# Turned x and the first gate weights in shared transfers, x itself later, in a two-block transformer kernel

## The chip, the cores and the metric

The kernel runs on one core of one Trainium2 chip. The metric is the device time of one execution in microseconds (us), lower is better.

## The reference

Two blocks run one after the other on 256 tokens of width 1024, in float32, each block with two layers. What the change touches is only the very first part, the first feed-forward part of the first layer of the first block:

```
h = x
h = h + 0.5 * swiglu(rmsnorm(h, ffn1_norm[0]), w_gate, w_up, w_down)

swiglu(x, w_gate, w_up, w_down) = (silu(x @ w_gate) * (x @ w_up)) @ w_down
rmsnorm(x, g) = x * rsqrt(mean(x * x) + 1e-6) * g
```

`w_gate` and `w_up` are 1024 x 2816, `w_down` is 2816 x 1024. After it come a mixer of three branches, a second feed-forward part, the second layer, and then the second block with mixers and feed-forward parts of its own.

## The kernel before

**Numbers.** Each float32 product is made of three TensorE passes. A matrix is split into a high half (the value rounded to the fast format, `fp32r`, by ScalarE) and a low half (the value minus the high half, by VectorE). The three matmuls are low weights by high x, high weights by high x, and high weights by low x.

**Weight units.** All weights come in units, numbered j in the order in which they are used. A unit is one transfer from DRAM by SyncE into `raw[j % 6]`; ScalarE writes the high half into `wh[j % 5]` (line 1850), VectorE the low half into `wl[j % 6]` (line 2062). `raw[i]` and `wl[i]` are the same memory, so the fetch of unit j waits until TensorE is done with unit j - 6, and the high half of unit j waits until it is done with unit j - 5 (`NL, NH = 6, 5`, line 29). A unit is used in two visits, one for each half of the tokens (t = 0 and 1).

**Written-out order.** One planner, the class `Plan`, writes a single list of items; each engine's program walks through that list and executes its own items in that order. So the order on an engine is the order of the list. `group` (line 511) makes the TensorE items of some units and calls `tick` after each visit. `tick` (line 477) does three things in order: it runs what was put off, it moves each of four lanes of generators one step (`pump`, line 459), and it calls `advance` (line 427), which appends fetches whose buffer has been given back, low halves for high halves already listed, and high halves. In the opening `advance` lists high halves only up to three units ahead of the unit in use:

```
            if self.head < 14 and self.nhi > self.head + 3:
                break
```

**The opening.** In the first column chunk (512 gate columns, then 512 up columns) the reduction over 1024 is cut into eight k-tiles of 128. Gate comes as units of 1, 1, 1, 1, 2, 2 k-tiles (units 0 to 5), up as units of 2, 2, 4 (units 6 to 8). Later chunks have units of four k-tiles; unit 9 is the first gate unit of the second chunk. Units 0 to 3 are "fresh" (line 1595): TensorE takes high by high as soon as both high halves are there, then the low half of x, then the low half of the weights. All other units wait for the low half of the weights first.

The first feed-forward part doesn't wait for the norm: x comes turned (features on partitions) in an array `xg`, which also holds the gain, and is scaled by the gain while it is split (lines 1844, 2055 and 2057, one "slot" for each k-tile). The roots of the mean squares are applied later, as a scale in silu (line 1858) and in the product with up (line 2069). They come from x in its plain layout (`h`, loaded at line 1476): ScalarE squares and sums it (line 1884), GpSimd makes the root (lines 1510 and 1514).

`start` (line 844) lists the opening: transfers of units 0 to 5 with `xg` in three pieces between them (slots 0 and 1, 2 and 3, 4 to 7), then x in its plain layout, the identity for transposes, 16 filler matmuls for TensorE (line 1641), then the splits of x and of units 0 to 4. `opening` (line 870) is a lane: after five steps it lists the squares and roots, 14 steps later the loads of constants by GpSimd (lines 1527 to 1532). `silu_t` (line 729) lists silu at once, behind the visit that ends the gate sum.

Of the kernel before, what the change touches and what calls it, by code (L numbers as in the profile page):

```python
# [17 lines left out]
P = 128  # L18
D = 1024
S = 256  # L20
# [8 lines left out]
NL, NH = 6, 5  # L29
# [38 lines left out]
class Memory:  # L68


    def __init__(self, nc, A, out, ctx):
        self.nc, self.A, self.out, self.ctx = nc, A, out, ctx
        self.sbuf()
        s = self.sem
# [17 lines left out]
        self.fill_set = s("fill_set")  # L92
        self.xt_landed = [s(f"xt_landed{i}") for i in range(3)]
        self.x0_high = s("x0_high")
# [45 lines left out]
    def sbuf(self):  # L140
# [11 lines left out]
        A = self.at  # L152
# [45 lines left out]
        o_g = [rt(8192), rt(8192)]  # L198
        self.GT = [A(f"G{i}", o_g[i], [P, 8 * S]) for i in range(2)]
        o_lane = [rt(3584) for _ in range(3)]  # L200
        self.fill = A("fill", o_g[0] + 4096, [P, P], F32R)
        self.xg = A("xg", o_g[1] - 32, [P, 8 + 8 * S])
        self.gcol = self.xg[:, 0:8]
        self.xT = self.xg[:, 8:].rearrange("p (s n) -> p s n", n=S)
        self.lS = [[A(f"lS{i}{j}", o_lane[i] + 1536 * j, [P, 384]) for j in range(2)] for i in range(3)]
# [86 lines left out]

    def halves(self, j):
        kt, n = self.unit(j)
        return self.raw[j % NL][:, 0:kt * n], self.wh[j % NH][:, 0:kt * n], self.wl[j % NL][:, 0:kt * n]

# [75 lines left out]
class Plan:  # L372
# [54 lines left out]
    def advance(self, most=NL):  # L427
        while self.fetched < self.total and (self.fetched < NL or self.fetched - NL in self.freed):
            j = self.fetched
            self.add("fetch", j=j, after=self.freed.get(j - NL))  # L430
            self.fetched += 1
        if self.held:
            return
        while self.nlo < self.nhi:
            self.add("low", j=self.nlo)
            self.nlo += 1
        while self.nhi < self.total and (self.nhi < NH or self.nhi - NH in self.freed) and self.nhi - self.nlo < most:
            if self.head < 14 and self.nhi > self.head + 3:
                break
            j = self.nhi  # L440
            self.add("high", j=j, after=self.freed.get(j - NH))
            self.nhi += 1
# [68 lines left out]
    def group(self, jobs, start=False, end=False):  # L511

        idx = [self.take(j["key"]) for j in jobs]
        for t, u in self.visits(len(jobs), start, end):
            j, job = idx[u], jobs[u]
            X, slots = job["X"], job["slots"]
            self.head = j
            self.split(j)
            need = self.need(X, slots, [t])
            if job["first"]:  # L520
                for b, _, _ in job["segs"]:
                    self.main_use[t, b] = self.use(2 * t + b)
            segs = [(self.main_use[t, b], c0, c1) for b, c0, c1 in job["segs"]]
            done = job["last"] or (t == 1 and job.get("sum", False))
            if t == 1 and job.get("cut"):
                for q in range(2):
                    use = self.side()
                    v = self.pe("tokens", j=j, t=t, X=X, slots=slots, segs=[(use, 256 * q, 256 * q + 256)], first=True,
                                stop=True, need=need)
                    job["cut"](q, v["p"], use)  # L530
                self.freed[j] = v["p"]
                self.tick()
                continue
            v = self.pe("tokens", j=j, t=t, X=X, slots=slots, segs=segs, first=job["first"],
                        stop=done, need=need, fresh=j < 4)
            if t == 1:
                self.freed[j] = v["p"]
            if X == "M":
                for s in slots:
                    self.m_free[s] = v["p"]  # L540
            if X == "X":
                self.x_free = v["p"]
            if done:
                job["epi"](t, v["p"], [u[0] for u in segs])
            self.tick()
# [151 lines left out]
    def ffn1(self, l, pre, after, loads):  # L697
# [6 lines left out]
        for n0, chunks, sizes in ((0, (512, 512, 512), (2, 4)), (1536, (512, 512, 256), (1, 4))):  # L704
            self.clear("M", range(12))
            slot, c0 = 0, n0
            for n in chunks:
# [6 lines left out]
                else:  # L714
                    parts = {gate: (4, 4), up: (4, 4)}
                    if opening and c0 == 0:
                        parts = {gate: (1, 1, 1, 1, 2, 2), up: (2, 2, 4)}
                    elif n == 256:
                        parts = {gate: (8,), up: (8,)}
# [9 lines left out]
    def silu_t(self, n, root):  # L729
        def epi(t, p, uses):  # L730
            while root and len(self.roots) < 2:
                self.pump()
            self.add("silu", i=t, p=p, use=uses[0], free=self.sg_free[t], n=n, root=root)
            self.sg_use[t] = uses[0]
        return epi

    def gate_w(self, q):
# [106 lines left out]
    def start(self):  # L844
# [4 lines left out]
        self.gain_n = 1  # L849
        for j in range(NL):  # L850
            self.add("fetch", j=j, after=None)
            if j in (0, 1, 3):
                self.add("load_turned", i=(j + 1) // 2)
        for t in range(2):
            self.add("load", t=t)
        self.add("load_ident")
        self.fetched = NL
        self.early = True
        self.pe("wake", n=16)
        self.x_free = -1  # L860
        for slots in ((0,), (1,), (2,), (3,), (4, 5), (6, 7)):
            for s in slots:
                self.add("xsplit", slot=s)
                for t in range(2):
                    self.ready["X", s, t] = ("x_low", s + 1)
            if slots[0] < 6:
                self.split_next()
        self.lanes[0].append(self.opening())

    def opening(self):  # L870

        for _ in range(5):
            yield
        for t in range(2):
# [3 lines left out]
            self.roots.append(self.next("rstd"))  # L878
        for _ in range(14):
            yield  # L880
# [583 lines left out]
def sp_program(e, m, plan):  # L1464

    sp = Engine(e, m, None)
    for it in plan.items:
# [11 lines left out]
        elif k == "load_turned":  # L1479
            a, b = ((0, 8 + 2 * S), (8 + 2 * S, 8 + 4 * S), (8 + 4 * S, 8 + 8 * S))[it["i"]]  # L1480
            e.dma_start(m.xg[:, a:b], m.A["xg"][:, a:b]).then_inc(m.xt_landed[it["i"]], 16)
# [7 lines left out]
def pool_program(e, m, plan):  # L1489
# [9 lines left out]
    for it in plan.items:  # L1499
# [23 lines left out]
        elif k == "wake":  # L1523
            e.memset(m.fill[:, :].bitcast(F32), 1.0).then_inc(m.fill_set, 1)
            e.memset(m.nhalf[:, :], -0.5).then_inc(m.half_set, 1)
        elif k == "consts":
            e.dma_start(m.mask[:, :], m.A["c_mask"]).then_inc(m.const_landed, 16)
            e.dma_start(m.freq[:, :], m.A["c_freq"]).then_inc(m.const_landed, 16)
# [51 lines left out]
def pe_program(e, m, plan):  # L1580
# [4 lines left out]
    for it in plan.items:  # L1585
        k, i, t, l, use = it["k"], it.get("i"), it.get("t"), it.get("l"), it.get("use")
        if k == "tokens":
# [7 lines left out]
            if it.get("fresh"):  # L1595
# [9 lines left out]
                pe.wait_ge(m.low_done, it["j"] + 1)  # L1605
                e.matmul(pb[b][:, :], xh[:, s, cols], lo[:, 0, :], start=False, stop=False).then_inc(m.pe_done, 1)
                continue
# [221 lines left out]
def act_program(e, m, plan):  # L1829
# [4 lines left out]
    for it in plan.items:  # L1834
# [6 lines left out]
        elif k == "xsplit" and it["slot"]:  # L1841
            s = it["slot"]
            a.wait_ge(m.xt_landed[min(s // 2, 2)], 16)
            e.activation(m.xh[:, s, :], m.xT[:, s, :], ACT.Copy, scale=m.gcol[:, s:s + 1]).then_inc(m.x_high, 1)
        elif k == "high":
            j = it["j"]
            raw, hi, lo = m.halves(j)
            a.wait_ge(m.raw_landed[j % NL], 16 * (j // NL + 1))
            a.pe(it["after"])
# [568 lines left out]
def layouts(inp):  # L2418
# [15 lines left out]
    for c in range(0, P, 32):  # L2434
# [5 lines left out]
    a["xg"] = np.concatenate([g["ffn1_norm"][0].reshape(8, P).T,  # L2440
                              g["x"][0].T.reshape(8, P, S).transpose(1, 0, 2).reshape(P, 8 * S)], 1)
    a.update(constants())
# [46 lines left out]
```

## Time and profile before

| | |
|---|---|
| median of 3 runs | 2051.63 us (2051.55 to 2051.82) |
| the profiled execution, its own time | 2051.74 us |
| its span | 2049.9 us |
| TensorE busy (matmul) | 2039.5 us, 99% of the span |
| VectorE busy | 1385.7 us, 68% |
| ScalarE busy | 1018.4 us, 50% |
| GpSimd busy | 89.8 us, 4% |
| moved by DMA | 377.20 MB, mean 184 GB/s |

The span is the profiler's record of one execution; the time of the same execution has 1.8 us more around it. Times in the rows are in us from the start of the span. PE is TensorE's matmul, PEld its weight load, DVE VectorE, ACT ScalarE, POOL GpSimd, SP SyncE; a q behind the name means the queue that issues its transfers. L1850 is line 1850 of the kernel. In a timeline, `x3` means that three instructions were merged, and the brackets tell how long the engine was idle before and what ended that.

### The profile page before, as it was taken

To read this page: it belongs to the slowest core of one execution; us is meant where nothing else is said; L and a number is where in the kernel's file an instruction comes from. 1 tells how busy PE (TensorE), PEld (TensorE's weight loads), DVE (VectorE), ACT (ScalarE), POOL (GpSimd) and SP (SyncE) were. 2 spreads that over 40 slices of the span, in tenths; PEclk is the share of its full clock that TensorE was granted. 3 is DMA by queue.
4 is the path that set the end of the run, shared out by engine and by line. 5 is a ranking of instruction groups with operands and counts; after the bars stand their busy time and mean duration, and the time that the engine had idled before them with its cause. 6 is when DMAs were issued, how large, how long until landed. Compare 5 with 4: busy or idle time off the path is not lost.

```text
span 2049.9 us, 25153 instructions
## 1 busy us (share of the span) xinstructions
PE 2039.5 (99%) x10364; PEld 1719.6 (84%) x10364; DVE 1385.7 (68%) x1626; ACT 1018.4 (50%) x1290; POOL 89.8 (4%) x131
## 2 busy tenths in 40 slices
PE   9999999999999999999999999999999999999998
PEld 7888888888888888888888888888888888888887
DVE  5655686775757566877575567657767667577675
ACT  6444576453444435675443465644444466444331
POOL 1001010000010001100100000000100000000000
PEclk9999999999999999999999999999999999999999
DMA  9655554465556556544656474555755645455552
GB/s 319 213 194 167 170 164 144 159 208 196 186 188 217 189 173 200 165 144 145 221 192 195 157 235 155 164 170 173 234 186 191 206 147 186 160 187 188 196 191 83
DMA packets 223729, 377.20 MB, mean 184 GB/s; under 512 B 6544, under 2 KB 109072, under 8 KB 223616
## 3 DMA queue, kind: packets, MB, share of 16 engines
q1 hardware_dynamic: 219792, 362.64, 53.7%
q0 software_dynamic: 3824, 12.97, 2.1%
q8 instruction: 82, 1.34, 0.3%
q14 instruction: 31, 0.25, 0.0%
HBM read 374.53 MB, written 1.05 MB: 183 GB/s over the span
## 4 chain that ended last, share of the span: by engine, by line
PE 96%; DVE 2%; ACT 1%; DMA 1%; issue 0%; POOL 0%; DVEq 0%; SPq 0%; ACTq 0%
PE pb L1613 64%; PE pb L1624 17%; PE pb L1627 9%; PE pb L1636 2%; DVE wl L2062 1%; PE pb L1682 1%; PE pb L1760 0%; DMA raw<-in_ffn_w_up_dram 0%; ACT wh L1850 0%; PE pb L1747 0%; PE pb L1824 0%; PE pb L1759 0%; DMA xg<-in_xg_dram 0%; PE pb L1739 0%; PE pb L1774 0%
## 5 line engine op out<-in xcount | busy, mean ns | idle before, releaser
L1850 ACT ACTIVATE wh<-raw 128x2048 fp32r<-128x2048 f32 (+4 forms) x351 | 658.3, 1876 | 627.2 <-PE pb L1613 250.5
L2062 DVE TENSOR_TENSOR wl<-raw,wh 128x2048 fp32r<-128x2048 f32 (+4 forms) x351 | 782.6, 2235 | 164.7 <-ACT wh L1850 164.3
L1613 PE MATMUL pb<-wh,x 128*128 128x512 f32 (+1 forms) x2224 | 676.3, 386 | 0.0
L1613 PEld LDWEIGHTS pb<-wh,x 128*128 128x128 f32 x2224 | 415.7, 188 | 80.9
L1613 PE MATMUL pb<-wl,x 128*128 128x512 f32 (+2 forms) x1112 | 439.0, 395 | 1.9 <-DVE wl L2062 1.8
L1624 PE MATMUL pb<-x,wh 128*128 128x512 f32 x1504 | 379.6, 394 | 0.0
L1624 PEld LDWEIGHTS pb<-x,wh 128*128 128x128 f32 x1504 | 271.6, 189 | 49.5
L1613 PE MATMUL pb<-wl,mh 128*128 128x512 f32 (+1 forms) x740 | 255.7, 391 | 0.0
L1613 PE MATMUL pb<-wh,ml 128*128 128x512 f32 (+1 forms) x740 | 253.7, 388 | 0.0
L1613 PE MATMUL pb<-wh,mh 128*128 128x512 f32 (+1 forms) x740 | 253.5, 388 | 0.0
L1613 PEld LDWEIGHTS pb<-wl,x 128*128 128x128 f32 x1112 | 209.0, 188 | 47.2 <-issue 3.7
L1627 PEld LDWEIGHTS pb<-x,wl 128*128 128x128 f32 x1504 | 205.2, 190 | 14.7
L1627 PE MATMUL pb<-x,wl 128*128 128x256 f32 x1504 | 209.7, 282 | 0.0
L1613 PEld LDWEIGHTS pb<-wh,ml 128*128 128x128 f32 x740 | 138.9, 188 | 28.9
L1613 PEld LDWEIGHTS pb<-wh,mh 128*128 128x128 f32 x740 | 139.0, 188 | 28.3
L1613 PEld LDWEIGHTS pb<-wl,mh 128*128 128x128 f32 x740 | 138.0, 188 | 26.9
L2107 DVE SCALAR_TENSOR_TENSOR h<-pb,h 128x512 f32<-128x512 f32 x72 | 48.1, 686 | 82.1 <-PE pb L1613 82.1
L2081 DVE TENSOR_REDUCE sg<-pb 128x256 f32<-128x512 f32 x102 | 70.1, 687 | 40.0 <-PE pb L1627 40.0
L2081 DVE TENSOR_REDUCE mn<-pb 128x256 f32<-128x512 f32 x54 | 37.1, 688 | 50.5 <-PE pb L1627 50.3
L1877 ACT ACTIVATE mh<-pb 128x512 fp32r<-128x512 f32 (+1 forms) x42 | 24.1, 583 | 59.9 <-PE pb L1636 59.9
L2102 DVE TENSOR_TENSOR ml<-pb,mh 128x512 fp32r<-128x512 f32 (+1 forms) x42 | 28.0, 675 | 37.3 <-ACT mh L1877 37.2
L1613 PE MATMUL pb<-wl,yph 128*128 128x512 f32 x128 | 51.4, 402 | 0.0
(361 smaller groups left out, 1590.1 us busy)
## 6 DMA issues: line engine op xcount, KB each, us to landing
raw<-in_w_in_dram SPq DMA_DIRECT2D x100, 1024.0 KB, 5.3
raw<-in_w_ff_dram SPq DMA_DIRECT2D x64, 1024.0 KB, 5.3
raw<-in_ffn_w_down_dram SPq DMA_DIRECT2D x44, 1024.0 KB, 4.9
raw<-in_ffn_w_up_dram SPq DMA_DIRECT2D x43, 1024.0 KB, 5.3
raw<-in_ffn_w_gate_dram SPq DMA_DIRECT2D x42, 1024.0 KB, 5.3
raw<-in_w_branch_dram SPq DMA_DIRECT2D x24, 1024.0 KB, 5.0
raw<-in_w_out_dram SPq DMA_DIRECT2D x16, 1024.0 KB, 5.0
raw<-in_w_in_dram SPq DMA_DIRECT2D x4, 832.0 KB, 4.4
```

Source lines behind the costliest of these rows:

```text
L1613: ins = e.matmul(pb[b][:, 0:c1 - c0], x[:, s, cols], w[:, n, c0:c1], start=(it["first"] and n == 0 and q == 0), stop=(it["stop"] and n == ...
L1624: e.matmul(bank[:, :], hi[:, s, c], m.x2[:, s, :, :].rearrange("p a s -> p (a s)"), start=(s == 0), stop=False, skip_group_check=True)
L1627: ins = e.matmul(bank[:, 0:S], lo[:, s, c], m.xh[:, s, :], start=False, stop=(s == 7), skip_group_check=True)
L1636: ins = e.transpose(bank[:, c * P:c * P + P], m.tile(it["src"], c), ident[:, :])
L1682: ins = e.transpose(bank[:, c * P:c * P + P], Sb[:, c * P:c * P + P], ident[:, :])
L1850: e.activation(hi, raw, ACT.Copy).then_inc(m.high_done, 1)
L1877: e.activation(hi, src, ACT.Copy).then_inc(m.turn_high, 1)
L2062: e.tensor_tensor(lo, raw, hi.bitcast(F32), ALU.subtract).then_inc(m.low_done, 1)
L2081: e.tensor_reduce(m.half(it["dst"], i), bank[:, :].rearrange("p (a s) -> p s a", a=2), AXX, ALU.add).then_inc(m.evac[use[0]], 1)
L2102: e.tensor_tensor(lo, src, hi.bitcast(F32), ALU.subtract).then_inc(m.evac[use[0]], 1)
L2107: e.scalar_tensor_tensor(o, bank[:, :], it["coef"], o, ALU.mult, ALU.add).then_inc(m.evac[use[0]], 1)
```

## The change

Turned x and the first gate weights are laid out together in DRAM: the array `xg` holds the gain, and then for each of the eight k-tiles 256 columns of turned x and 512 columns of gate weights. Eight transfers bring one such pair each (the first with the gain). Gate is now eight units of one k-tile, all "fresh"; up is four units of two. So the units of the first chunk are 0 to 7 (gate) and 8 to 11 (up), and unit 12 is the first gate unit of the second chunk. Gate weights of units 0 to 7 stay in `xg`, not in `raw`, which makes `xg` larger; it now covers the memory of the constants, and so GpSimd waits for the last split of x and of these weights before it loads them. The load of x in its plain layout and of the identity moves from `start` into the lane `opening`, behind ten steps; the squares and roots come seven steps after it, the constants eight steps after those. The first two silus are put on lanes, three steps behind. There are 13 filler matmuls in place of 16.

```diff
-        self.xt_landed = [s(f"xt_landed{i}") for i in range(3)]
+        self.xt_landed = [s(f"xt_landed{i}") for i in range(8)]
...
-        self.xg = A("xg", o_g[1] - 32, [P, 8 + 8 * S])
+        self.xg = A("xg", o_g[1] - 32, [P, 8 + 8 * (S + 512)])
         self.gcol = self.xg[:, 0:8]
-        self.xT = self.xg[:, 8:].rearrange("p (s n) -> p s n", n=S)
+        xw = self.xg[:, 8:].rearrange("p (s n) -> p s n", n=S + 512)
+        self.xT, self.w0 = xw[:, :, 0:S], xw[:, :, S:]
...
     def halves(self, j):
+
         kt, n = self.unit(j)
-        return self.raw[j % NL][:, 0:kt * n], self.wh[j % NH][:, 0:kt * n], self.wl[j % NL][:, 0:kt * n]
+        raw = self.w0[:, j, :] if j < 8 else self.raw[j % NL][:, 0:kt * n]
+        return raw, self.wh[j % NH][:, 0:kt * n], self.wl[j % NL][:, 0:kt * n]
...
-            if self.head < 14 and self.nhi > self.head + 3:
+            if self.head < 17 and self.nhi > self.head + 3:
...
-                        stop=done, need=need, fresh=j < 4)
+                        stop=done, need=need, fresh=j < 8)
...
-                        parts = {gate: (1, 1, 1, 1, 2, 2), up: (2, 2, 4)}
+                        parts = {gate: (1,) * 8, up: (2, 2, 2, 2)}
...
         def epi(t, p, uses):
-            while root and len(self.roots) < 2:
-                self.pump()
-            self.add("silu", i=t, p=p, use=uses[0], free=self.sg_free[t], n=n, root=root)
+            item = dict(i=t, p=p, use=uses[0], free=self.sg_free[t], n=n, root=root)
+            if t in self.sg_use:
+                self.add("silu", **item)
+            else:
+                self.lanes[1 + t].append(self.first_silu(item))
             self.sg_use[t] = uses[0]
         return epi
+
+    def first_silu(self, item):
+
+        for _ in range(3):
+            yield
+        assert len(self.roots) == 2
+        self.add("silu", **item)
...
-        for j in range(NL):
-            self.add("fetch", j=j, after=None)
-            if j in (0, 1, 3):
-                self.add("load_turned", i=(j + 1) // 2)
+        for j in range(8):
+            self.add("load_turned", i=j)
+        self.fetched = 8
+        self.early = True
+        self.pe("wake", n=13)
+        self.x_free = -1
+        for s in range(8):
+            self.add("xsplit", slot=s)
+            for t in range(2):
+                self.ready["X", s, t] = ("x_low", s + 1)
+            if s < 5:
+                self.split_next()
+        self.lanes[0].append(self.opening())
+
+    def opening(self):
+
+        for _ in range(10):
+            yield
         for t in range(2):
             self.add("load", t=t)
         self.add("load_ident")
-        self.fetched = NL
-        self.early = True
-        self.pe("wake", n=16)
-        self.x_free = -1
-        for slots in ((0,), (1,), (2,), (3,), (4, 5), (6, 7)):
-            for s in slots:
-                self.add("xsplit", slot=s)
-                for t in range(2):
-                    self.ready["X", s, t] = ("x_low", s + 1)
-            if slots[0] < 6:
-                self.split_next()
-        self.lanes[0].append(self.opening())
-
-    def opening(self):
-
-        for _ in range(5):
+        for _ in range(7):
             yield
         for t in range(2):
             for b in range(2):
                 self.square(t, b)
             self.add("root", t=t, sq=self.count["squared"])
             self.roots.append(self.next("rstd"))
-        for _ in range(14):
+        for _ in range(8):
             yield
...
         elif k == "load_turned":
-            a, b = ((0, 8 + 2 * S), (8 + 2 * S, 8 + 4 * S), (8 + 4 * S, 8 + 8 * S))[it["i"]]
+            s, n = it["i"], S + 512
+            a, b = (8 + n * s if s else 0), 8 + n * (s + 1)
             e.dma_start(m.xg[:, a:b], m.A["xg"][:, a:b]).then_inc(m.xt_landed[it["i"]], 16)
...
         elif k == "consts":
+            po.wait_ge(m.x_low, 8)
+            po.wait_ge(m.low_done, 8)
             e.dma_start(m.mask[:, :], m.A["c_mask"]).then_inc(m.const_landed, 16)
...
-            a.wait_ge(m.xt_landed[min(s // 2, 2)], 16)
+            a.wait_ge(m.xt_landed[s], 16)
...
-            a.wait_ge(m.raw_landed[j % NL], 16 * (j // NL + 1))
+            if j < 8:
+                a.wait_ge(m.xt_landed[j], 16)
+            else:
+                a.wait_ge(m.raw_landed[j % NL], 16 * ((j - 8) // NL + 1))
...
     a["xg"] = np.concatenate([g["ffn1_norm"][0].reshape(8, P).T,
-                              g["x"][0].T.reshape(8, P, S).transpose(1, 0, 2).reshape(P, 8 * S)], 1)
+                              np.concatenate([g["x"][0].T.reshape(8, P, S), g["ffn1_w_gate"][0, :, 0:512].reshape(8, P, 512)],
+                                             2).transpose(1, 0, 2).reshape(P, 8 * (S + 512))], 1)
```

## Rows read from the trace of the kernel before

**Rows 1.** The page: busy time, share of the span and instructions of each engine.
```profile
PE 2039.5 (99%) x10364; PEld 1719.6 (84%) x10364; DVE 1385.7 (68%) x1626; ACT 1018.4 (50%) x1290; POOL 89.8 (4%) x131
```

**Rows 2.** Waits of TensorE, whole span: who for whom, total us, times, longest.
```profile
PE pb L1613 <- DVE wl L2062: 1.8, 2, 1.3
```

**Rows 3.** Timeline of TensorE: start, us, engine, line, operation [idle before].
```profile
0.98 5.54 PE L1641 MATMUL pb<-fill 128*128 128x512 f32 x16 [0.98 <-POOL fill L1524]
6.35 0.40 PE L1602 MATMUL pb<-wh,x 128*128 128x512 f32 x1
...
7.08 0.50 PE L1606 MATMUL pb<-wl,x 128*128 128x512 f32 x1
...
13.69 0.50 PE L1613 MATMUL pb<-wl,x 128*128 128x512 f32 x1 [1.32 <-DVE wl L2062]
...
25.41 0.50 PE L1613 MATMUL pb<-wl,x 128*128 128x512 f32 x1 [0.50 <-DVE wl L2062]
25.75 0.62 PE L1613 MATMUL pb<-wh,x 128*128 128x512 f32 x2
...
30.99 0.39 PE L1613 MATMUL pb<-wl,x 128*128 128x512 f32 x1
```

**Rows 4.** SyncE's issues, and us from issue to landing of the same ones.
```profile
4.49 0.95 SPq L1473 DMA_DIRECT2D raw<-in_ffn_w_gate_dram  x1
...
raw<-in_ffn_w_gate_dram SPq DMA_DIRECT2D x1, 512.0 KB, 8.2
...
11.04 0.37 SPq L1473 DMA_DIRECT2D raw<-in_ffn_w_up_dram  x1
...
raw<-in_ffn_w_up_dram SPq DMA_DIRECT2D x1, 1024.0 KB, 9.8
```

**Rows 5.** Windows; the last two columns are DMA share and GB/s.
```profile
3.25:5.25 2.00, 2.00 (x8) 1.59 (x7) 0.00 (x0) 0.63 (x1) 0.00 (x0) 1.00 0.86 187
5.25:7.25 2.00, 1.89 (x9) 1.25 (x8) 1.66 (x4) 1.11 (x2) 0.00 (x0) 1.00 0.94 325
7.25:12.90 5.65, 5.12 (x22) 3.89 (x22) 4.24 (x9) 4.60 (x10) 0.00 (x0) 1.00 1.04 409
12.90:20.84 7.94, 7.15 (x31) 5.83 (x32) 5.11 (x6) 7.40 (x14) 4.92 (x10) 1.00 1.05 387
```

**Rows 6.** Timeline of ScalarE in the opening.
```profile
3.49 0.63 ACT L1850 ACTIVATE wh<-raw 128x512 fp32r<-128x512 f32 x1 [1.27 <-DMA raw<-in_ffn_w_gate_dram]
5.55 0.51 ACT L1844 ACTIVATE x<-xg 128x256 fp32r<-128x256 f32 x1 [1.44 <-DMA xg<-in_xg_dram]
...
13.08 1.04 ACT L1850 ACTIVATE wh<-raw 128x1024 fp32r<-128x1024 f32 x1
14.03 0.62 ACT L1884 ACTIVATE xn<-h 128x512 f32<-128x512 f32 x1
...
16.41 0.19 ACT L1884 ACTIVATION_READ_ACCUMULATOR xn<-h 128x1 f32 x1
...
19.25 1.28 ACT L1858 ACT_TABLE_LOAD   x1
20.54 0.69 ACT L1858 ACTIVATE sg<-pb,st 128x512 f32<-128x512 f32 x1
21.13 1.91 ACT L1850 ACTIVATE wh<-raw 128x2048 fp32r<-128x2048 f32 x1
```

**Rows 7.** Timeline of VectorE.
```profile
5.94 0.48 DVE L2057 SCALAR_TENSOR_TENSOR x<-xg,x 128x256 fp32r<-128x256 f32 x1
6.34 0.68 DVE L2062 TENSOR_TENSOR wl<-raw,wh 128x512 fp32r<-128x512 f32 x1
...
23.07 2.29 DVE L2062 TENSOR_TENSOR wl<-raw,wh 128x2048 fp32r<-128x2048 f32 x1 [2.58 <-ACT wh L1850]
```

**Rows 8.** DMA queues from 17.6 to 20.84 us: the one that moved packets.
```profile
q1 hardware_dynamic: 628, 1.25, 105.0%
```

**Rows 9.** Timeline of GpSimd.
```profile
17.09 0.56 POOL L1514 TENSOR_TENSOR st<-st,nhalf 128x1 f32<-128x1 f32 x1
```

More of the change, by code:

```diff
@@ L1605, in pe_program @@
                 pe.wait_ge(m.low_done, it["j"] + 1)
-                e.matmul(pb[b][:, :], xh[:, s, cols], lo[:, 0, :], start=False, stop=False).then_inc(m.pe_done, 1)
+                e.matmul(pb[b][:, :], xh[:, s, cols], lo[:, 0, :], start=False, stop=it["stop"]).then_inc(m.pe_done, 1)
                 continue
```

## The prediction

> **What bounds the kernel now.** I read the page first: TensorE is busy for 2039.5 of 2049.9 us [rows 1]. So only time in which TensorE stands idle or turns on filler can be won. The waits of TensorE over the whole span put a size on it: 1.8 us in two waits for low halves of weights, the longer 1.3 [rows 2]. TensorE's timeline shows where [rows 3]. Sixteen filler matmuls run up to the first real one at 6.35; the third waits until 7.08; unit 4 starts at 13.69 and unit 8 at 25.41, each behind its low halves. From there matmuls of 512 columns follow one another unbroken. Unit 8 holds 24 of them and unit 9 starts at 30.99, so one takes (30.99 - 25.75) / 23 = 0.228 us, and a k-tile (two token halves, three matmuls each) 1.37 us. The opening has 16 k-tiles, 21.9 us of work; without a stall it would have had to start at 30.99 - 21.9 = 9.1. That 9.1 is the number that the change must lower: whatever it takes off the start of the first unit of the second column chunk comes off the end, if nothing stalls later.
>
> What sets it is transfers. Unit 8 was issued at 11.04 and needed 9.8 us, so it landed at 20.84 [rows 4]. In transfer order 6212 KB are then in: gate columns with turned x 3076, x itself and the identity 1088, up weights 2048. The rates of the windows are 187 GB/s from 3.25 to 5.25, then 325, 409 and 387 [rows 5]. After the landing: ScalarE's high half at 21.13, VectorE's low half at 23.07, TensorE at 25.41 [rows 3, 6, 7].
>
> **The change part by part.** Unit numbers: gate 0 to 7, up 8 to 11 (two k-tiles each), the second chunk's first unit is 12 (9 before).
>
> *First pair.* Before, weight tile 0 landed at 3.49 and the first piece of x at 5.55, where ScalarE's idle time ends [rows 6]. The new first transfer has 388 KB, between the 256 and the 516 KB that were in at these two times: 3.5 to 5.6; by bytes I take 4.5. Behind it ScalarE needs 0.63 for the high half, VectorE 0.48 and 0.68 for the low halves of x and weights [rows 6, 7]. Before, from x's landing to the matmul with the low half took 7.08 - 5.55 = 1.5, so that one can run at 6.0. Thirteen fillers end three times 0.228 earlier than sixteen, near 5.7, and don't hold it up.
>
> *Pairs 1 to 7.* The bytes up to pair 7 are those that were in when old unit 5 landed, 4.49 + 8.2 = 12.7 [rows 4]. By the same curve pairs 1 to 4 land near 6.6, 7.7, 8.6 and 9.6, about 1 us apart, faster than TensorE's 1.37; ScalarE (0.51 and 0.63) and VectorE (0.48 and 0.68) keep up. Pair 1 costs a stall of about 1 us; tile 4 ends near 13.4. Now the order written in start(): the x halves of slots 5, 6 and 7 stand on ScalarE ahead of unit 5's high half, since only five high buffers exist. Unit 5, in since about 10.7, waits for pair 7 at 12.7. Then 0.4 (x half, to the next start), 0.63 and 0.7: its low half is ready at 14.5, its first two matmuls run before that, and the tile counts from 14.0. The dense start is thus 14.0 - 5 x 1.37 = 7.2, 1.9 us better than 9.1.
>
> *Up units.* Each is fetched when the unit six before it is done, since raw and low halves share buffers: units 8 to 10 are issued near 10.8, 12.1 and 13.4, while earlier transfers are still flowing, and land near 14, 15.4 and 16.8 by the 387 GB/s. TensorE wants them at 18.2, 20.9 and 23.6. No stall; old unit 8's wait is gone.
>
> *x itself.* I counted the lane steps. opening() yields ten times, so x and the identity are issued behind the fetch of unit 10 and *ahead* of unit 11's. So again 6212 KB stand before unit 11's landing: 20.84, as before (software-queue packets first show behind 20.84 [rows 8], so nothing else is removed from that time).
>
> *Roots and silu, moved.* The squares come after unit 8's second token half, in ScalarE's order right behind unit 11's high half. Then silu 0, silu 1, and only then unit 12's high half: each silu waits three lane steps, and the step that adds silu 1 adds unit 12's high half behind it. Before, the squares filled ScalarE's wait for the first up unit (14.03 to 16.60). Here they stand in a chain that begins with a landing. The durations, all from [rows 6]: high half of unit 11, start to next start, 0.95 (13.08 to 14.03); four squares with their reads 2.57; table load 1.28, then 0.01; silu to the next start 0.59 (20.54 to 21.13), twice. From 20.86: 21.81, 24.38, 25.68, 26.28, 26.87. GpSimd's second root ended at 17.65, 3.62 after the squares' start [rows 9]; here at 25.4, ahead of both silus' need. Unit 12 has landed by then (20.84 + 1 MB at 387 GB/s = 23.6). High half to low half 1.94 and low half to matmul 2.34 (21.13, 23.07, 25.41): TensorE starts unit 12 at 31.15.
> It wants it at 7.2 + 21.9 = 29.1. So it stalls about 2 us there, and refilling costs 0.11 more (0.34 from 25.41 to 25.75 instead of 0.228 [rows 3]). Position 31.26 against 30.99: 0.27 us later. The 1.9 us won in front are given back at one point.
>
> The Trainium skill (ScalarE: Activation LUTs, What ACT_TABLE_LOAD costs) adds a drain of about 1.38 us to each switch of the table. By it the sum would be 1.4 us more. The trace disagrees: load at 19.25, 1.28 long, silu at 20.54 [rows 6]; I take the row.
>
> *Afterwards.* Unit 13's low half: VectorE goes on from 31.0, ready at 33.3, wanted at 36.7. The constants start on GpSimd behind the second root, at 25.4 instead of 17.65, and share the engines with units 14 and 15 instead of 9 and 10; the bytes in by 36 are the same, and unit 14 is wanted only near 42. Their new waits hold long before. The three more units, their semaphores and shifted buffers cost nothing that TensorE sees while it is fed ahead by a unit. I put 0 here; against a shifted small stall I keep 0.5 to either side, the shorter wait of [rows 3].
>
> **Sum.** The profiled execution took 2051.74 for its span of 2049.9; the median of the runs is 2051.63. With +0.3 on the median: 2051.9. Bounds: unit 11 lands 0.7 earlier (the weak first rates gain from longer rows) or 0.8 later, and every tenth of it goes through, since that chain has no slack.
>
> About 0.2% (4.1 us) is what a measurement of this kernel tells from no change. All that can be won here is less: even without any stall behind the first pair, counting from 6.0 - 0.45, 9.1 - 5.5 = 3.6.
>
> **Rivals.**
> 1. *The gain holds.* ScalarE's chain is shorter than I say, because my count of the steps is off by one and unit 12's high half goes ahead of the silus, or because squares slip into the wait for unit 11. Then TensorE's own pace rules: 29.1 instead of 30.99, 2049.7; with half of it 2050.7. For it: 1.9 us are won in front. Against it: the written order. Chance 0.2.
> 2. *Slower, by the packed array.* Place: the first eight transfers. In 3.25 to 5.25 the rate was 187 GB/s [rows 5], with x rows among the first. If weights packed with them flow like that for longer, pair 7 and unit 11 land later, and each us of that is one at the end. At 325 GB/s (row 5.25:7.25) instead of 409 in 7.25 to 12.9, 2.3 MB take 1.5 us more: 2053.4. To be slower by 4.1 pair 7 must land 3.8 later: from the span's start on, 3.15 MB / 16.5 = 191 GB/s instead of 3.15 / 12.7 = 248. Against it: turned x came in the same odd pitch within the 409. The Trainium skill (DMA: Bandwidth & Descriptors, How a descriptor splits into AXI transactions) says that a descriptor not starting at a multiple of 256 B fetches bytes that it throws away; the packed rows are 24,608 B apart, so most weights now start so. Chance 0.1.
> 3. *Slower, by a longer ScalarE chain.* Place: between squares and silu 0. If the chain drains before the load, or the roots come a table load later, the end moves 1.3 us (the load's own length): 2053.2. Chance 0.08.
> 4. *The change doesn't do what it says*: x doesn't come behind all the up units, as counted. This is in the forecast. Were it behind unit 11, that unit would land 2.8 us sooner, the squares would wait for x instead, and unit 12 would start at the same place within 1 us: 2051 to 2053.
>
> **Numbers.** Forecast 0.62, within 2051.2 to 2052.7. Rivals 1, 2 and 3 make it 2049.8 to 2053.4. Only rival 2 at its far end reaches the 0.2% upward; nothing named reaches it downward. Faster 0.02, same 0.94, slower 0.04.
>
> **What would show it.** Right: first real matmul between 5 and 6; unit 5's high half directly behind slot 7's x half; no wait for units 8 to 11; then ScalarE in the order squares, table load, two silus, high half, and one wait of TensorE of about 2 us for a low half, ending near 31.2. Wrong: unit 12 started near 29, or pair 7 landing outside 11.5 to 14, or a second stall beyond unit 12.

## The result: 4.3 us slower

The changed kernel takes 2056.03 us (median of 14 runs, 2054.85 to 2057.68) against 2051.69 before; the ratio is 1.0021, with a 95% interval of 1.0014 to 1.0028. That is 4.3 us slower, just over the 0.2% bound, where +0.3 was forecast and 2053.4 was the top of the range. The spread is new too: 2.8 us between the runs, where the kernel before keeps within 0.4.

The page of the profiled execution (2056.28 us) shows a span 4.6 us longer than before and TensorE 2.3 us *busier* with three matmuls fewer ([rows 1]). A busier engine with less work runs slower somewhere.

```profile
span 2054.5 us, 25158 instructions
...
PE 2041.8 (99%) x10361; PEld 1721.7 (84%) x10361; DVE 1386.3 (67%) x1629; ACT 1019.2 (50%) x1293; POOL 90.0 (4%) x131
```

The waits of TensorE over the whole span: the two waits of [rows 2] are replaced by a single one.

```profile
PE pb L1627 <- DVE wl L2079: 4.2, 1, 4.2
PE pb L1655 <- POOL fill L1536: 1.0, 1, 1.0
```

TensorE's timeline, around the start and around unit 12 (answers to [rows 3]):

```profile
0.98 5.91 PE L1655 MATMUL pb<-fill 128*128 128x512 f32 x13 [0.98 <-POOL fill L1536]
6.70 0.61 PE L1616 MATMUL pb<-wh,x 128*128 128x512 f32 x1
...
33.13 0.77 PE L1627 MATMUL pb<-wl,x 128*128 128x512 f32 x1 [4.20 <-DVE wl L2079]
33.69 1.06 PE L1627 MATMUL pb<-wh,x 128*128 128x512 f32 x2
34.54 0.63 PE L1627 MATMUL pb<-wl,x 128*128 128x512 f32 x1
...
40.89 0.60 PE L1650 MATMUL pb<-ident,mn 128*128 128x128 f32 x4
```

Unit 12 was forecast at 31.15 and starts at 33.13. Behind it matmuls are 0.43 us apart (33.69 to 34.54 is two), where 0.228 was usual. The first transposes, at the same place of the work, come at 40.89 and came at 36.44 before: 4.45 us later. Of these 33.13 - 30.99 = 2.14 are unit 12's late start, and (40.89 - 33.13) - (36.44 - 30.99) = 2.31 are the slow stretch. The windows name both causes (last three columns: granted clock, DMA share, GB/s; answers to [rows 5]):

```profile
3.00:11.00 8.00, 8.00 (x28) 6.33 (x27) 5.85 (x12) 5.09 (x10) 0.00 (x0) 1.00 0.98 362
11.00:13.00 2.00, 2.00 (x11) 1.65 (x10) 1.26 (x3) 1.51 (x4) 0.00 (x0) 1.00 0.34 45
13.00:16.00 3.00, 3.00 (x15) 2.49 (x14) 1.93 (x5) 2.13 (x4) 0.00 (x0) 1.00 0.85 250
16.00:22.70 6.70, 6.70 (x32) 5.53 (x31) 3.67 (x3) 2.12 (x2) 0.00 (x0) 1.00 1.04 400
31.00:38.00 7.00, 4.87 (x12) 3.91 (x13) 7.00 (x5) 3.37 (x2) 0.69 (x4) 0.51 1.04 371
```

The granted clock is 0.51 from 31 to 38, so TensorE was at its lower level, 1.2 GHz instead of 2.4. And the transfers, at 362 GB/s up to 11, fall to 45 GB/s for two us and to 250 for three more. Cut finer, that is two dips: nothing moves from 11.5 to 12.0, then it is back at 401 GB/s from 13.5 to 14.0, and down again to 94 from 14.5 to 15.0. SyncE's timeline says why the first one comes:

```profile
0.73 3.93 SPq L1493 DMA_DIRECT2D xg<-in_xg_dram  x8
11.28 3.09 SPq L1484 DMA_DIRECT2D raw<-in_ffn_w_up_dram  x3
14.41 0.94 SPq L1487 DMA_DIRECT2D h<-in_x_dram  x2
...
16.05 0.46 SPq L1484 DMA_DIRECT2D raw<-in_ffn_w_up_dram  x1
```

The eight pairs are issued by 4.7. The next issue, unit 8, is at 11.28, when TensorE is done with unit 2, since it lands in that unit's buffer. By then the DMA engines have nothing left. Units 9 and 10 are gated in the same way and follow 1.36 us apart, at TensorE's pace; which of this makes the second dip was not tested.

ScalarE's timeline (answers to [rows 6]) and the line of VectorE behind it (it merges units 12 and 13):

```profile
4.13 0.63 ACT L1867 ACTIVATE wh<-xg 128x512 fp32r<-128x512 f32 x1 [1.91 <-DMA xg<-in_xg_dram]
...
12.00 0.51 ACT L1858 ACTIVATE x<-xg 128x256 fp32r<-128x256 f32 x1 [0.42 <-DMA xg<-in_xg_dram]
12.41 1.66 ACT L1867 ACTIVATE wh<-xg 128x512 fp32r<-128x512 f32 x3
...
22.77 1.06 ACT L1867 ACTIVATE wh<-raw 128x1024 fp32r<-128x1024 f32 x1 [3.12 <-DMA raw<-in_ffn_w_up_dram]
23.74 0.61 ACT L1901 ACTIVATE xn<-h 128x512 f32<-128x512 f32 x1
...
26.09 0.19 ACT L1901 ACTIVATION_READ_ACCUMULATOR xn<-h 128x1 f32 x1
26.30 1.28 ACT L1875 ACT_TABLE_LOAD   x1
27.59 1.27 ACT L1875 ACTIVATE sg<-pb,st 128x512 f32<-128x512 f32 x2
28.75 3.71 ACT L1867 ACTIVATE wh<-raw 128x2048 fp32r<-128x2048 f32 x2
```

```profile
30.69 4.49 DVE L2079 TENSOR_TENSOR wl<-raw,wh 128x2048 fp32r<-128x2048 f32 x2 [5.60 <-ACT wh L1867]
```

This is the forecast order to the instruction: unit 5's high half (12.41) directly behind slot 7's x half, and behind unit 11 four squares, table load, two silus, unit 12's high half. From 22.77 to TensorE's start at 33.13 the chain takes 10.36 us; forecast was 31.15 - 20.86 = 10.29. The chain was right. It began 1.9 us late.

### The profile page after: what moved, and what is told of

Same layout as the page of the kernel before. It is cut to its first block, busy times and chain, and to the rows that moved or that the text cites. A ratio compares the mean times of both kernels' runs of the same rounds, so it can differ in the third digit from the quotient of the medians.

```text
span 2054.5 us, 25158 instructions
## 1 busy us (share of the span) xinstructions
PE 2041.8 (99%) x10361; PEld 1721.7 (84%) x10361; DVE 1386.3 (67%) x1629; ACT 1019.2 (50%) x1293; POOL 90.0 (4%) x131
## 4 chain that ended last, share of the span: by engine, by line
PE 96%; DVE 2%; ACT 1%; issue 0%; POOL 0%; DVEq 0%; ACTq 0%; POOLq 0%
PE pb L1627 64%; PE pb L1638 16%; PE pb L1641 9%; PE pb L1650 2%; DVE wl L2079 1%; PE pb L1696 1%; PE pb L1774 0%; PE pb L1655 0%; ACT wh L1867 0%; PE pb L1761 0%; PE pb L1838 0%; PE pb L1773 0%; PE pb L1753 0%; PE pb L1788 0%; DVE lS L2262 0%; PE pb L1616 0%
## 5 line engine op out<-in xcount | busy, mean ns | idle before, releaser
L1867 ACT ACTIVATE wh<-raw 128x2048 fp32r<-128x2048 f32 (+1 forms) x346 | 653.8, 1891 | 626.5 <-PE pb L1627 244.6
L2079 DVE TENSOR_TENSOR wl<-raw,wh 128x2048 fp32r<-128x2048 f32 (+1 forms) x346 | 777.6, 2253 | 165.6 <-ACT wh L1867 165.1
L1627 PE MATMUL pb<-wh,x 128*128 128x512 f32 (+2 forms) x2208 | 672.8, 386 | 0.0
```

The lines of the kernel that those rows point to most:

```text
L1627: ins = e.matmul(pb[b][:, 0:c1 - c0], x[:, s, cols], w[:, n, c0:c1], start=(it["first"] and n == 0 and q == 0), stop=(it["stop"] and n == ...
L1867: e.activation(hi, raw, ACT.Copy).then_inc(m.high_done, 1)
L2079: e.tensor_tensor(lo, raw, hi.bitcast(F32), ALU.subtract).then_inc(m.low_done, 1)
```

## The experiments

The kernel before, measured beside each of these runs, gave medians of 2051.65 to 2051.74. In the table, times are in us from the span's start in each run's profile, medians in us. The profiled executions of runs 1 and 3 are the slowest of their ten (2055.31 and 2056.19), that of run 2 is the second slowest (2052.20), so landings read from them lie at the late end. "Chain" runs from unit 11's high half to unit 12's first matmul.

| run | unit 11 high | unit 12 starts | chain | TensorE's wait for unit 12 | first transposes | median |
|---|---|---|---|---|---|---|
| before (units 8, 9) | 21.13 | 30.99 | | none | 36.44 | 2051.69 |
| the change | 22.77 | 33.13 | 10.36 | 4.20 | 40.89 | 2056.03 |
| fillers in the stall | 24.04 | 34.41 | 10.37 | 0.88 | 39.95 | 2053.80 |
| x behind the pairs | 20.55 | 30.91 | 10.36 | 1.26 | 36.49 | 2051.74 |
| 8 fillers at the start | 23.03 | 33.38 | 10.35 | 4.97 | 40.92 | 2055.03 |
| up units not gated | 17.03 | no wait | | none | 33.52 | 2049.46 |
| no squares | 26.32 | 34.70 | | 1.41 | 40.24 | 2056.70 |
| no squares, constants held | 21.91 | 29.99 | 8.08 | 1.52 | 35.54 | 2051.31 |
| order moved | 22.60 | 30.16 | | 0.67 | 35.88 | 2051.26 |
| order moved, constants held | 22.52 | no wait | | none | 35.14 | 2050.49 |
| not gated, 8 fillers | 16.90 | no wait | | none | 33.41 | 2048.81 |

**1. Does the clock carry half of the loss?** Fillers keep TensorE busy in the stall.

```diff
             self.head = j
+            if j == 12 and t == 0:
+                self.pe("refill", n=18)
             self.split(j)
...
+        elif k == "refill":
+            for c in range(it["n"]):
+                ins = e.matmul(pb[7][:, :], m.xh[:, 0, 0:P], m.x2[:, 0, :, :].rearrange("p a s -> p (a s)"), start=True,
+                               stop=True)
+            ins.then_inc(m.pe_done, 1)
```

> The changed kernel with 18 filler matmuls on TensorE (of x, results unused) in front of unit 12, so that TensorE isn't idle in the long stall; everything else is as in the change. Theory (the loss of 4.3 us is two things: unit 12 starts 2.1 us late, and its 4.2 us stall drops the clock to the lower level, which costs another 2.3): unit 12 still starts near 33.1, the granted clock stays at 1.00 from 31 to 38, unit 12 takes 5.5 us instead of 7.8, the time falls by 2.3 to about 2053.7 and the runs spread less than 2.8 us. Rival (the clock is a side effect and the loss sits in waits spread over the kernel): within 0.5 us of 2056.0.

Measured: 2053.80 (2052.97 to 2055.31), ratio to before 1.0010 (1.0001 to 1.0020). TensorE's timeline and the window of 31 to 38:

```profile
29.29 4.24 PE L1662 MATMUL pb<-x 128*128 128x512 f32 x18
34.41 0.47 PE L1629 MATMUL pb<-wl,x 128*128 128x512 f32 x1 [0.88 <-DVE wl L2086]
...
39.95 0.60 PE L1652 MATMUL pb<-ident,mn 128*128 128x128 f32 x4
```

```profile
31.00:38.00 7.00, 6.12 (x28) 4.78 (x27) 6.03 (x5) 5.97 (x4) 1.94 (x7) 1.00 1.05 375
```

The clock stays at 1.00, and from unit 12's start to the transposes it takes 5.54 instead of 7.76. The median falls by 2.2, as expected. In this profile unit 11 landed even later (24.04), so the start of unit 12 is later than in the change; it is the faster clock that makes the run faster. The spread fell only from 2.8 to 2.3, so most of it isn't the clock's. The landings are the likely source, but that is not shown.

**2. Is it the empty queue?** x itself goes behind the pairs, where it fills the gap; nothing else moves.

```diff
         for j in range(8):
             self.add("load_turned", i=j)
+        for t in range(2):
+            self.add("load", t=t)
+        self.add("load_ident")
...
-        for _ in range(10):
-            yield
-        for t in range(2):
-            self.add("load", t=t)
-        self.add("load_ident")
-        for _ in range(7):
+        for _ in range(17):
             yield
```

> The change with x itself and the identity issued right behind the eight pairs instead of behind unit 10; squares, roots and silus keep their places. Theory (unit 11 lands late because the transfer queue runs empty between 11 and 13 us, while the up units' fetches wait for TensorE): the queue stays full, unit 11 lands near 20.3 instead of 22.75, ScalarE's chain of 10.3 us behind it is unchanged, unit 12 starts near 30.6, its stall is about 1.7 us and the clock stays up: about 2051.3. Rival (only ScalarE's order matters, not the landing): unit 12 starts near 33 as in the change, 2056. Rival (a stall of 1.7 us drops the clock too): 2053.6.

Measured: 2051.74, ratio 1.0000 (0.9991 to 1.0009), spread 1.1. Windows, ScalarE's line of unit 11's high half, and TensorE's timeline:

```profile
11.00:13.00 2.00, 2.00 (x11) 1.58 (x9) 1.21 (x3) 1.53 (x4) 0.00 (x0) 1.00 1.03 418
13.00:16.00 3.00, 3.00 (x14) 2.14 (x13) 1.91 (x4) 1.05 (x3) 0.00 (x0) 1.00 1.03 372
```

```profile
20.55 1.06 ACT L1865 ACTIVATE wh<-raw 128x1024 fp32r<-128x1024 f32 x1 [0.71 <-DMA raw<-in_ffn_w_up_dram]
```

```profile
30.91 0.47 PE L1625 MATMUL pb<-wl,x 128*128 128x512 f32 x1 [1.26 <-DVE wl L2077]
...
36.49 0.60 PE L1648 MATMUL pb<-ident,mn 128*128 128x128 f32 x4
```

418 GB/s where the change has 45; unit 11 at 20.55, 2.2 earlier; the chain unchanged at 10.36; unit 12 2.2 earlier; no slow stretch. One moved load takes back the whole 4.3 us. A new wait of 0.77 us appears at 18.48, at unit 8, which now lands behind x; it only takes time from the stall at unit 12. This run is also nearly the kernel of my forecast: the same bytes without a gap, and it measures within 0.2 us of the 2051.9 predicted.

**3. How much do the fillers at the start matter?**

```diff
-        self.pe("wake", n=13)
+        self.pe("wake", n=8)
```

> The change with 8 fillers instead of 13 at the start. In the change the 13 fillers ran at 0.43 us each and held the first real matmul until 6.70 though its operands were there at 4.8. Theory (the fetches of the up units follow TensorE's progress): the first real matmul is near 4.9, units 8 to 11 are issued 1 to 1.8 us earlier, the empty stretch of the queue shrinks, unit 11 lands 1 to 1.8 us earlier and unit 12 starts as much earlier, the stall stays about 4 us long and the clock still drops: 2054.2 to 2055. Rival (the start doesn't matter since ScalarE's chain binds): 2056 and a longer stall.

Measured: 2055.03, ratio 1.0017 (1.0007 to 1.0026). TensorE's timeline:

```profile
0.98 3.78 PE L1655 MATMUL pb<-fill 128*128 128x512 f32 x8 [0.98 <-POOL fill L1536]
4.77 0.79 PE L1616 MATMUL pb<-wh,x 128*128 128x512 f32 x1
...
33.38 0.77 PE L1627 MATMUL pb<-wl,x 128*128 128x512 f32 x1 [4.97 <-DVE wl L2079]
...
40.92 0.60 PE L1650 MATMUL pb<-ident,mn 128*128 128x128 f32 x4
```

The first real matmul moves from 6.70 to 4.77 and the up units are issued from 10.16 instead of 11.28, but in this profile unit 11 isn't in sooner (23.03). The stall only grows to 4.97. The median gained 1.0 us, at the slow end of the expectation; that the landing moved by 1 to 1.8 was not seen in the one execution profiled, the slowest of the ten. The run shows something else. At 10.16 the pairs were still flowing (369 GB/s from 10.0 to 10.5), and yet from 11 to 12 the rate was 119 GB/s, and 87 in run 8, issued at 10.18. So an issue that comes just before the queue is empty does not prevent the dip either.

**4. All up units without a gate.** Weight tiles of units 0 to 7 use a quarter of each low buffer. Units 8 to 11 can land in its upper half without waiting for TensorE.

```diff
+        for j in range(8, 12):
+            self.add("fetch", j=j, after=None)
-        self.fetched = 8
+        self.fetched = 12
...
-        return self.raw[j % NL][:, 0:kt * n].rearrange("p (k n) -> p k n", n=n), src
+        o = 1024 if j < 12 else 0
+        return self.raw[j % NL][:, o:o + kt * n].rearrange("p (k n) -> p k n", n=n), src
...
-        raw = self.w0[:, j, :] if j < 8 else self.raw[j % NL][:, 0:kt * n]
+        o = 1024 if j < 12 else 0
+        raw = self.w0[:, j, :] if j < 8 else self.raw[j % NL][:, o:o + kt * n]
```

> The change with units 8 to 11 landing in the upper halves of their raw buffers, issued right behind the pairs without waiting for TensorE; x itself keeps its place and so comes behind all up units. Theory: the queue stays full, unit 11 lands near 17.4, x itself near 20.2; the squares start then, table load, silus and unit 12's high and low half follow (2.6 + 1.3 + 1.2 + 1.9 + 2.3 us), unit 12 starts near 29.6, stall under 1 us, clock stays up: about 2050.3. Rival (x itself still lands near 21, or the packed rows are slow): unit 12 near 31, 2051.7.

Measured: 2049.46, ratio 0.9989 (0.9980 to 0.9999): faster than before, by 0.1%. SyncE's and ScalarE's timelines, and TensorE's waits over the whole span:

```profile
4.52 2.53 SPq L1488 DMA_DIRECT2D raw<-in_ffn_w_up_dram  x4
7.09 2.08 SPq L1491 DMA_DIRECT2D h<-in_x_dram  x2
```

```profile
17.03 1.06 ACT L1871 ACTIVATE wh<-raw 128x1024 fp32r<-128x1024 f32 x1 [0.29 <-DMA raw<-in_ffn_w_up_dram]
18.31 0.63 ACT L1905 ACTIVATE xn<-h 128x512 f32<-128x512 f32 x1 [0.22 <-DMA h<-in_x_dram]
...
21.00 1.28 ACT L1879 ACT_TABLE_LOAD   x1
...
23.45 1.92 ACT L1871 ACTIVATE wh<-raw 128x2048 fp32r<-128x2048 f32 x1
```

```profile
PE pb L1659 <- POOL fill L1540: 1.0, 1, 1.0
PE pb L1792 <- DVE zv L2343: 0.4, 2, 0.2
```

Units 8 to 11 and x are issued by 9.2. Unit 11 is in at 17.0, x at 18.3, not 20.2 as I expected, since x no longer stands behind gated fetches either. The chain now begins so early that its 10 us are hidden, and no wait for weights is left.

**5. and 8. Are the four squares really in the chain?** They and the roots are left out, and so the roots' scale; all transfers stay.

```diff
-        for t in range(2):
-            for b in range(2):
-                self.square(t, b)
-            self.add("root", t=t, sq=self.count["squared"])
-            self.roots.append(self.next("rstd"))
+        self.roots = [0, 1]
...
-                                     epi=self.silu_t(n, opening) if b == 0 else self.up_t(slot, n, opening))
+                                     epi=self.silu_t(n, False) if b == 0 else self.up_t(slot, n, False))
```

> The changed kernel without the four squares and two roots of the first norm (silu and the product with up then take 1.0 in place of the root, so this part of the computation is left out); all transfers as in the change. Theory (ScalarE's chain between unit 11's landing and unit 12's high half is 2.6 us too long, and every us of it is one of stall): unit 11 still lands near 22.8, unit 12 starts near 30.6, the stall is about 1.7 us, the clock stays up, so the gain is 2.5 us of stall and 2.3 us of clock: about 2051.3. Rival (unit 12 waits for its own landing, squares are hidden): 2056.

Measured: 2056.70, ratio 1.0024 (1.0014 to 1.0034), the figure of the rival. ScalarE's line of unit 11 and GpSimd's first issue:

```profile
26.32 1.06 ACT L1863 ACTIVATE wh<-raw 128x1024 fp32r<-128x1024 f32 x1 [7.13 <-DMA raw<-in_ffn_w_up_dram]
```

```profile
15.39 0.77 POOL L1537 DMA_DIRECT2D mask<-in_c_mask_dram  x1 [14.43 <-DVE wl L2075]
```

This was a bad experiment, not a verdict. GpSimd works in order, and with the roots gone nothing held the constants' loads: they were issued at 15.39 instead of 27.34, and unit 11 landed at 26.3. TensorE then stalled at unit 11 itself, for 3.01 us up to 28.69, and once more at unit 12 for 1.41. So it was run again with one wait more:

```diff
             po.wait_ge(m.low_done, 8)
+            po.wait_ge(m.high_done, 13)
```

> The run without squares and roots again (that part of the computation is left out), with GpSimd's constants held back until unit 12's high half is made. In the first such run nothing held GpSimd any more: it issued the constants at 15.4 instead of 27.3, they shared the transfer engines, and unit 11 landed at 26.3 instead of 22.8, so that run told nothing of the squares. Theory: now unit 11 lands near 22.8, high half, table load, two silus and unit 12's halves follow, unit 12 starts near 30.6, stall about 1.7 us, clock up: about 2051.3. Rival (squares hidden): 2056.

Measured: 2051.31, ratio 0.9999 (0.9990 to 1.0009). ScalarE's and TensorE's timelines:

```profile
21.91 1.06 ACT L1864 ACTIVATE wh<-raw 128x1024 fp32r<-128x1024 f32 x1 [3.08 <-DMA raw<-in_ffn_w_up_dram]
...
25.60 1.92 ACT L1864 ACTIVATE wh<-raw 128x2048 fp32r<-128x2048 f32 x1 [0.23 <-DMA raw<-in_ffn_w_gate_dram]
```

```profile
29.99 0.47 PE L1624 MATMUL pb<-wl,x 128*128 128x512 f32 x1 [1.52 <-DVE wl L2076]
...
35.54 0.60 PE L1647 MATMUL pb<-ident,mn 128*128 128x128 f32 x4
```

The chain is 8.08 us. Without squares it is 10.36 - 2.57 = 7.8, and 0.23 is a wait for unit 12's landing. Unit 11 was in 0.86 us sooner here and TensorE ready for unit 12 0.46 sooner (28.47 instead of 28.93), so of the 2.68 us that the stall lost, 2.28 are the chain's. With a stall of 1.52 the clock stays up.

**6. and 9. Squares and silus into ScalarE's idle time.** On top of run 2, the squares go ahead of unit 8's high half and the silus ahead of unit 11's, by the numbers of lane steps alone.

```diff
-        for _ in range(17):
+        for _ in range(10):
             yield
...
-        for _ in range(3):
+        for _ in range(1):
             yield
         assert len(self.roots) == 2
...
-        for _ in range(8):
+        for _ in range(15):
             yield
         self.early = False
```

> The run with x itself behind the pairs (2051.74), with only ScalarE's order changed: squares and roots go ahead of unit 8's high half, both silus ahead of unit 11's. Theory (the 10.3 us chain holds unit 12; its pieces fit into ScalarE's waits for landings): the wait at unit 12 (1.26 us) goes, the one at unit 8 (0.74) grows by about 0.5 because four squares end at 16.6 and unit 8 is in at 16.1: about 2050.9. Rival (order doesn't matter, transfers rule): 2051.7. Rival (the constants, now started ten us sooner on GpSimd, slow unit 12's landing): 2052.

Measured: 2051.26, ratio 0.9998 (0.9988 to 1.0007), with a spread of 2.3: half a us better than run 2, which its interval doesn't tell apart. ScalarE's timeline says what took the chain's place (units 11 and 12):

```profile
22.60 1.05 ACT L1865 ACTIVATE wh<-raw 128x1024 fp32r<-128x1024 f32 x1
25.77 1.92 ACT L1865 ACTIVATE wh<-raw 128x2048 fp32r<-128x2048 f32 x1 [2.12 <-DMA raw<-in_ffn_w_gate_dram]
```

Unit 12 is late itself now: 2.12 us of idle time for its transfer, beside constants that go out at 17.1 as soon as the roots are made. The same hold as in run 8 takes that away:

> The run with x itself behind the pairs and squares and silus moved ahead on ScalarE (2051.26), with the constants held back until unit 12's high half is made. In that run unit 12 landed at 25.8, 2.1 us after ScalarE was ready for it, beside constants issued from 17.1 on. Theory (the constants' traffic is the last wait there): unit 12 lands near 23.5, its wait on TensorE (0.67 us) goes, 2050.4 to 2050.8. Rival (the traffic is no part of it): 2051.3.

Measured: 2050.49, ratio 0.9994 (0.9985 to 1.0003), spread 0.6. Units 11 and 12 follow one another with no wait:

```profile
22.52 2.95 ACT L1866 ACTIVATE wh<-raw 128x1024 fp32r<-128x1024 f32 x2
```

What TensorE still waits for is unit 8, 1.35 us at 18.68: its high half starts at 16.31, behind the squares and 0.23 us of waiting for its landing.

**7. The best of these**, run 4 with 8 fillers.

> The run with up units landing without a wait for TensorE (2049.46), with 8 fillers instead of 13. Theory (with nothing late behind it, the start binds): the first real matmul moves from 5.9 to 4.8, real matmuls take over the time that fillers filled, partly at the lower clock, and tile 5 waits for ScalarE as the x halves of slots 5 to 7 stand before it: 0.4 to 1 us faster, about 2048.8. Rival (unit 5's high half behind pair 7 binds anyway): 2049.4.

Measured: 2048.81, ratio 0.9987 (0.9977 to 0.9997), 2.8 us faster than before and 7.2 faster than the change. TensorE's first real matmul is at 4.77, and the first transposes at 33.41. That is only 0.11 ahead of run 4 in the profiles; the medians differ by 0.65 and the two profiled executions by 0.59. The rest of that difference isn't there yet at 810 us and is there at 1310, far from what was edited. So the theory that the start is worth 0.4 to 1 us is not shown: the profiles bear out 0.1 of it.

## Why the prediction was wrong

- *Where the time is decided.* Right in the change. The whole difference arises before the first transposes: 4.45 of the span's 4.6 us.
- *The lane steps and the order.* Right, to the instruction: x ahead of unit 11, squares behind it, unit 12's high half behind silu 1. The chain of 10.3 us was right within 0.1, in four runs.
- *First pair.* Landing 4.5 forecast, 4.13 measured. But "Thirteen fillers end three times 0.228 earlier than sixteen, near 5.7, and don't hold it up" was wrong: they took 5.91 us and held the first real matmul to 6.70, though its high halves were there at 4.8. I had taken the last fillers' distance, 0.228, for all that were removed. The distance of the first ones is 0.43, and how many of them are slow differs from execution to execution: 13 fillers took 5.91, 5.65, 5.52 and 5.07 us in runs of the same opening.
- *The dense start.* 7.2 forecast. TensorE was ready for unit 12 at 33.13 - 4.20 = 28.93, so it measures 28.93 - 21.9 = 7.0. That this fits is luck in part: the fillers held the start back, and the two waits forecast behind it (pair 1, and unit 5 at 14.0) did not come.
- *Pairs 1 to 7.* Pair 7 in at 12.0, forecast 12.7. The rival of slow packed rows is gone: 362 GB/s from 3 to 11.
- *"Issued near 10.8, 12.1 and 13.4, while earlier transfers are still flowing."* **This is the step that failed.** The pairs' packets were through by 11.5, earlier than I thought, and the first gated fetch went out at 11.28, later than I thought. The queue ran empty; two us at 45 GB/s and three at 250 are 2 x (400 - 45) + 3 x (400 - 250) KB/us = 1.2 MB short, 2.9 us at the 400 GB/s that follow. Less the 0.7 that the pairs were early, this is unit 11's delay of 1.9 within 0.3. The sentence "again 6212 KB stand before unit 11's landing: 20.84, as before" holds only for a queue that never waits. I had the last pair landing at 12.7 and the next issue at 10.8, and took two us of margin for enough. But an issue into an empty queue needs time of its own: unit 8's 512 KB landed 3.6 us after theirs. And my premise, "while earlier transfers are still flowing", would not have been enough had it held: in runs 3 and 8 it did, with issues at 10.16 and 10.18, and the rate still fell to 119 and 87 GB/s from 11 to 12. Run 2, with the gap filled, gives back 4.3 us.
- *The clock.* **Missing from the sum.** A stall of about 2 us was forecast and no change of clock. With 4.20 us of stall the granted clock fell to half, and the work behind it cost 2.31 more (run 1 takes back 2.2). So a landing 1.9 us late cost 4.3 us, where "every tenth of it goes through" allowed 1.9. My slower rival had the place nearly right (unit 11 lands late, each us one at the end) with another mechanism, and stopped at 2053.4 for the same reason.
- *Afterwards.* Right: 0.15 us between the transposes and the end. Over all runs this part differs from the kernel before by -0.2 to +0.5 us (+0.5 in run 2), so agreements within less than that say little.
- *The signs.* None of the three named under "Wrong" came. Of those under "Right" two failed: the first real matmul was at 6.70 instead of between 5 and 6, and the wait was 4.20 us instead of about 2.
- *The Trainium skill's drain behind a table load* (ScalarE: Activation LUTs, What ACT_TABLE_LOAD costs): again no drain; load at 26.30, silu at 27.59.

The Trainium skill (TensorE: Matmul & The Clock Gate, HAM oscillation) says that long waits for data between matmuls put TensorE back to the lower clock in real kernels. The trace agrees for the stalls of 4.20 and 4.97 us here, and for 3.01 us in run 5 (granted clock 0.50 from 30 to 32); I had left it out of the sum.

What stays open: why the landing of unit 11 differs by more than 1 us between executions of one opening (22.77 in the change, 24.04 in run 1; 23.03 in run 3 and 21.91 in run 8, whose first gated issues are only 0.02 us apart). Kernels with the gap spread by about 2 us or more (the change 2.8, runs 1, 3, 5 and 8 2.3, 2.0, 1.9 and 3.0, the last by one execution of 2053.63), and of those without it runs 2, 4, 7 and 9 only by 1.1, 1.2, 1.1 and 0.6; but run 6 has no gap and spreads by 2.3. The gap alone doesn't settle it.

## What to carry to other kernels

When transfers are merged or moved ahead, ask of the first one behind them what its issue waits for. If it waits for the engine that the transfers feed, the queue can run dry, and the gap is paid at the next landing that something waits for. Count bytes for a landing time only after checking that each issue comes well before the queue is empty: an issue less than a us before that still left a dip here, a megabyte queued behind the pairs (run 2) left none. And price a stall of TensorE twice, once for its length and once for the work behind it at half clock if it is long: here stalls of 1.3 to 1.5 us cost only themselves, one of 4.20 us cost 2.3 more and one of 4.97 cost 2.1 more (7.54 from unit 12's start to the transposes, where the kernel before has 5.45).

Work that one moves behind others on an engine may have been what held a third engine back. Without the roots GpSimd's constants went out 12 us sooner and cost more than the squares had.

## What the runs showed of the hardware

- Granted clock: still 1.00 behind stalls of 1.26, 1.35, 1.41 and 1.52 us, about 0.5 behind stalls of 3.01, 4.20 and 4.97. Behind the stall of 3.01, in run 5, it was still 1.00 when work began again at 28.69 and fell after 29. In the change it reads 1.00 up to 31, is at half from then on, and matmuls are back at 0.228 us at 38.2, five us after work began again.
- Fillers of 512 columns at the start took 0.45 to 0.47 us each in the change and in run 3 (13 in 5.91, 8 in 3.78), while the granted clock reads 1.00 in the windows of that time. The distance of the matmuls shows the clock there, the column doesn't.
- A DMA queue that has run empty and is fed one gated transfer at a time doesn't come back at full rate for good: in the change 401 GB/s from 13.5 to 14.0, then 94 from 14.5 to 15.0 with the DMA engines busy for 0.78 of the time, 250 on the mean of 13 to 16; from 16 on 400.
